# One chip, two blocks of a network: the statistics between a block's end and the next, taken together, and the second attention's ends reordered

## What is computed

```python
def rmsnorm_2(x, g):
    xf = x.astype(jnp.float32)
    y = xf * lax.rsqrt(jnp.mean(xf * xf, axis=-1, keepdims=True) + EPS)
    return (y * g.astype(jnp.float32)).astype(x.dtype)
...
    h = rmsnorm_2(x, g_pre[l, 0]) * (1 + sc1) + sh1
    x = x + 0.5 * gt1 * rmsnorm_2(swiglu(h, w_gu1[l], w_dn1[l]), g_post[l, 0])

    h = rmsnorm_2(x, g_pre[l, 1]) * (1 + sc2) + sh2
    y = token_mixer(h, w_in[l], w_a2[l], b_a[l], b_f[l], g_gla[l], w_pa[l], w_pb[l], w_out[l])
    x = x + gt2 * rmsnorm_2(y, g_post[l, 1])

    h = rmsnorm_2(x, g_pre[l, 2]) * (1 + sc3) + sh3
    x = x + 0.5 * gt3 * rmsnorm_2(swiglu(h, w_gu2[l], w_dn2[l]), g_post[l, 2])
```

## Time and profile before

| | |
|---|---|
| median of 3 runs | 2352.78 us (2352.03 to 2357.11) |
| profiled execution, its own time | 2360.18 us |
| span in the profile, mean granted clock | 2358.0 us, 0.982 |
| PE busy | 2306.4 us, 98% |
| DVE, ACT, POOL busy | 42%, 38%, 44% |
| DMA | 263.95 MB, mean 112 GB/s |

### The profile page before, as it was taken

The page is one execution under the profiler, slowest core; times in us unless marked ns, Lnnn a source line. Parts: engine busy times, 40 slices in busy tenths (PEclk is TensorE's granted clock), DMA queues, the critical chain, the costliest instruction groups (busy, mean ns, idle before and its releaser), DMA issues.

```text
span 2358.0 us, 33517 instructions
## 1 busy us (share of the span) xinstructions
PE 2306.4 (98%) x10816; PEld 1904.4 (81%) x10816; DVE 982.0 (42%) x1616; ACT 897.8 (38%) x1621; POOL 1041.5 (44%) x792
## 2 busy tenths in 40 slices
PE   8999999999999999999999999999999899999997
PEld 7888888888888888888888778888677688888886
DVE  6899885446514214100113135555765425110112
ACT  4334653333222333332332354445555443332331
POOL 3455653454444443444454443333222353444443
PEclk8999999999999999999998999999999999999998
DMA  4333443338837532333332223335112431333331
GB/s 150 93 98 103 144 131 123 99 115 296 270 94 243 154 89 77 97 98 94 98 94 59 81 81 113 108 111 173 53 52 59 139 94 54 94 98 98 94 98 58
DMA packets 129338, 263.95 MB, mean 112 GB/s; under 512 B 14240, under 2 KB 14368, under 8 KB 128608
## 3 DMA queue, kind: packets, MB, share of 16 engines
q1 hardware_dynamic: 119520, 236.51, 33.7%
q10 hardware_dynamic: 9728, 26.25, 2.9%
HBM read 250.02 MB, written 12.58 MB: 111 GB/s over the span
## 4 chain that ended last, share of the span: by engine, by line
PE 67%; issue 19%; POOL 8%; DVE 4%; ACT 1%; DMA 0%; POOLq 0%; ACTq 0%; DVEq 0%
PE bank L973 22%; PE bank L974 21%; PE bank L975 21%; POOL wlo L406 8%; PE bank L1084 1%; DVE bank L1591 1%; PE bank L1108 1%; DVE G L1764 1%; DVE G L1774 1%; PE bank L1048 0%; PE bank L1092 0%; PE bank L1068 0%; DMA cols<-d_cols 0%; DVE bank L1662 0%; PE bank L1076 0%
## 5 line engine op out<-in xcount | busy, mean ns | idle before, releaser
L406 POOL TENSOR_TENSOR wlo<-raw,whi 128x512 fp32r<-128x512 f32 x750 | 992.5, 1329 | 1219.9 <-ACT whi L478 1219.0
L973 PE MATMUL bank<-a_hi,whi 128*128 128x512 f32 x1928 | 763.3, 396 | 10.2 <-POOL wlo L406 8.4
L975 PE MATMUL bank<-a_lo,whi 128*128 128x512 f32 x1928 | 751.9, 390 | 0.0
L974 PE MATMUL bank<-a_hi,wlo 128*128 128x512 f32 x1928 | 751.5, 390 | 0.0
L478 ACT ACTIVATE whi<-raw 128x512 fp32r<-128x512 f32 x750 | 468.9, 627 | 706.4 <-PE bank L975 629.2
L973 PEld LDWEIGHTS bank<-a_hi,whi 128*128 128x128 f32 x1928 | 362.7, 188 | 91.6 <-POOL wlo L406 10.0
L975 PEld LDWEIGHTS bank<-a_lo,whi 128*128 128x128 f32 x1928 | 362.6, 188 | 76.5
L974 PEld LDWEIGHTS bank<-a_hi,wlo 128*128 128x128 f32 x1928 | 363.0, 188 | 75.8 <-issue 1.4
L973 PE MATMUL bank<-b_hi,whi 128*128 128x512 f32 x852 | 336.1, 394 | 0.6 <-DVE b_lo L1729 0.3
L974 PE MATMUL bank<-b_hi,wlo 128*128 128x512 f32 x852 | 332.5, 390 | 0.0
L975 PE MATMUL bank<-b_lo,whi 128*128 128x512 f32 x852 | 332.5, 390 | 0.0
(11 more groups left out here) (245 smaller groups left out, 1860.9 us busy)
## 6 DMA issues: line engine op xcount, KB each, us to landing
raw<-d_stream SPq DMA_DIRECT2D x750, 256.0 KB, 2.6
G<-d_ada SPq DMA_DIRECT2D x72, 512.0 KB, 4.6
spill_rv<-tmp ACTq DMA_DIRECT2D x32, 256.0 KB, 2.0
G<-spill_rv ACTq DMA_DIRECT2D x6, 1024.0 KB, 7.3
G<-d_x ACTq DMA_DIRECT2D x4, 512.0 KB, 5.5
spill_ga<-sq ACTq DMA_DIRECT2D x8, 256.0 KB, 3.7
G<-spill_ga ACTq DMA_DIRECT2D x1, 2048.0 KB, 8.2
G<-d_x ACTq DMA_DIRECT2D x1, 2048.0 KB, 13.4
```

The source lines that it names most:

```text
L406: pool.tensor_tensor(wlo[:, s % SRING, :], raw[:, s % RING, :], whi[:, s % SRING, :].bitcast(F32), ALU.subtract).then_inc(lo_done, 1)
L973: pe.matmul(out_ps, w_hi, hi[:, k, :], start=first and q == 0, stop=False)
L974: pe.matmul(out_ps, w_lo, hi[:, k, :], start=False, stop=False)
L975: mm = pe.matmul(out_ps, w_hi, lo[:, k, :], start=False, stop=last and q == len(ks) - 1)
```

## The change

With y scaled by a per-feature weight w and by the root r1 of its own norm, the new x is x + r1 w y. The sum of its squares over the features is S(x x) + 2 r1 S(x w y) + r1 r1 S(w y w y). So the kernel after takes three sums while y's tiles come: S(y y) as before, S(x w y) and S(w y w y); S(x x) it keeps from the turn before (`X_SUM`). Per tile there are a second square on ACT (`weighted_square`) and on DVE a product and two additions (`cross`). PE sums six tiles of 512 positions into `AUX` and bank 6 (`sums_between`), and `roots` makes both roots, one behind the other. PE broadcasts both (`two_roots`), and `next_block` adds the residual and makes the operands in one loop over k. `residual` stays for the last block. `add_pairs`, the squares of x and the sums over pairs are gone in both turns.

At the start of the second attention the products for the second half (`by_r(1)`) move behind the first `tmp`, the first quotients from m = 3 to m = 6, and `qk_half(15)` from m = 5 to m = 7. At its end the gate loads are cut into halves, the first issued behind the last scores instead of the last output, and `tick("pb")` goes ahead of the waits and the sigmoids.

```diff
-        SQ8, PAIRS, SQ_FIRST = tiles(8 * T, KD), tiles(16 * T, 4), tiles(S0, KD)
+        SQ_FIRST = tiles(S0, KD)
         SQ_ACC = tmp[:, 1, :]
+        CA, BA, CROSS, GSQ = G[:, 8 * T:9 * T], G[:, 9 * T:10 * T], tiles(10 * T, 2), tiles(12 * T, 2)
+        X_SUM, ROOT1, ROOT2, SUM_T = small[:, 5, 8:12], small[:, 4, 8:12], small[:, 4, 12:16], small[:, 6, 8:12]
...
-            def add_pairs(norm):
-                for j in range(4):
-                    pool.wait_ge(sq_ready, 8 * norm + 2 * j + 2)
-                    pool.tensor_tensor(PAIRS[:, j, :], SQ8[:, 2 * j, :], SQ8[:, 2 * j + 1, :], ALU.add)\
-                        .then_inc(pair_ready, 1)
             def add_up(norm, k):
...
                 else:
                     to = PLAN[stage][0] + (AHEAD if at else 0)
                     low_run(at, to)
-                    if norm != "n1":
-                        add_pairs(NORM[norm])
                     at = to
...
+            def weighted_square(b, m):
+                if m > 1:
+                    act.wait_ge(gsq_added, 6 * b + max(m - 2, 1))
+                act.activation(GSQ[:, m % 2, :], Y[:, m, :], ACT.Square, scale=derived[:, 3 + b, m:m + 1])\
+                   .then_inc(gsq_ready, 1)
             def round_a(fill, val, shift=None, name=None):
...
                     if norm is not None:
                         wait_evac(act, name, 0, m)
                         square(norm, m, (X if norm in (NORM["n2"], NORM["nf"]) else Y)[:, m, :])
+                    if norm == NORM["post1"]:
+                        weighted_square(0, m)
             def ffn(n, norm):
...
             ffn(2, NORM["post1"])
-            for k in range(KD):
-                act.wait_ge(x_ready, KD + k + 1)
-                pair_square(k, X[:, k, :])
...
                         wait_used(act, "qkb", 0, 31)
                     operand_hi(s - (STEPS - 7))
+            act.wait_ge(fox_s, UNITS)
+            act.dma_start(GB2[:, 4:8, :], spill_rv[:, 3 * KD:3 * KD + 4, :]).then_inc(ld_b2[0], 16)
             act.wait_ge(fox_o, STEPS)
-            act.dma_start(GB2[:, 4:8, :], spill_rv[:, 3 * KD:3 * KD + 4, :]).then_inc(ld_gb, 16)
-            act.dma_start(GB2[:, 0:4, :], spill_rv[:, 3 * KD + 4:4 * KD, :]).then_inc(ld_gb, 16)
-            act.dma_start(GA2[:, :, :], spill_rv[:, 2 * KD:3 * KD, :]).then_inc(ld_ga, 16)
+            act.dma_start(GA2[:, 0:4, :], spill_rv[:, 2 * KD:2 * KD + 4, :]).then_inc(ld_g2[0], 16)
             operand_hi(KD - 1)
-            act.wait_ge(ld_ga, 32)
-            act.wait_ge(ld_gb, 32)
+            act.dma_start(GB2[:, 0:4, :], spill_rv[:, 3 * KD + 4:4 * KD, :]).then_inc(ld_b2[1], 16)
+            act.dma_start(GA2[:, 4:8, :], spill_rv[:, 2 * KD + 4:3 * KD, :]).then_inc(ld_g2[1], 16)
             for m in range(KD + 1):
                 if m < KD:
+                    tick("pb", 0, 2 * m)
+                    if m % 4 == 0:
+                        act.wait_ge(ld_g2[m // 4], 16)
+                        act.wait_ge(ld_b2[m // 4], 16)
                     act.activation(GA2[:, m, :], GA2[:, m, :], ACT.Sigmoid).then_inc(gate2, 1)
                     act.activation(gb2(m), gb2(m), ACT.Sigmoid).then_inc(gate2, 1)
-                    tick("pb", 0, 2 * m)
                 if m:
                     act.wait_ge(b_val, 2 * KD + m)
                     act.activation(b_hi[:, m - 1, :], tmp[:, (m - 1) % 2, :], ACT.Copy).then_inc(b_hi_w, 1)
...
                 act.activation(Y[:, m, :], bank_of("wout", m)[:, :], ACT.Copy).then_inc(evac_of("wout", m), 1)
                 wait_evac(act, "wout", 0, m)
                 square(NORM["post2"], m, Y[:, m, :])
-            for k in range(KD):
-                act.wait_ge(x_ready, 2 * KD + k + 1)
-                pair_square(k, X[:, k, :])
+                weighted_square(1, m)
             round_a("hf3", 40, lambda k: mods[:, 48 + k:49 + k], "gu3a")
...
+                for tt in range(4):
+                    mm = pe.matmul(sums[:, at + tt:at + tt + 1], value[:, tt * P:(tt + 1) * P], ones[:, 0:1],
+                                   start=first and tt == 0, stop=tt == 3, skip_group_check=True)
+                return mm
+            def sums_between(b, norm):
+                pe.wait_ge(sq_summed, 8 * norm + KD - 1)
+                sum_at(AUX, 0, SQ_ACC, True)
+                pe.wait_ge(cross_ready, 3 * b + 2)
+                sum_at(bank[6], 0, BA, True)
+                sum_at(bank[6], 4, CA)
+                pe.wait_ge(sq_ready, 8 * norm + KD)
+                sum_at(AUX, 0, sq[:, (KD - 1) % 2, :]).then_inc(sq_summed, 1)
+                pe.wait_ge(cross_ready, 3 * b + 3)
+                sum_at(bank[6], 4, CROSS[:, (KD - 1) % 2, :])
+                pe.wait_ge(gsq_ready, KD * (b + 1))
+                sum_at(bank[6], 0, GSQ[:, (KD - 1) % 2, :]).then_inc(between, 1)
+            def two_roots(n):
+                keep_warm(12)
+                broadcast(n, src=ROOT1)
+                keep_warm(14)
+                broadcast(n + 1, src=ROOT2, dst=bank[6])
+                keep_warm(22)
...
                     sum_both(KD - 1)
+                elif n == 2:
+                    sums_between(0, norm)
                 else:
                     sum_up(norm)
...
-            broadcast(7, warm=8)
-            keep_warm(26)
-            sum_pairs(1, "pre2")
-            broadcast(8, warm=8)
-            keep_warm(10)
+            two_roots(7)
             def row_panel(name, i, k, ops):
...
                     scores(1)
-                if m < 6:
-                    qk_half(10 + m)
+                if m < 5 or m == 7:
+                    qk_half(10 + min(m, 5))
             pe.wait_ge(ld_v, 32)
...
             stage8("pb", OPA, opa, FILL_A["ob"], 2)
             for m in range(KD):
                 tile8("wout", 0, m, OPB, opb, FILL_B["merged"], m == 0)
-            sum_up(NORM["post2"])
-            broadcast(9, warm=8)
-            keep_warm(26)
-            sum_pairs(2, "pre3")
-            broadcast(10, warm=8)
-            keep_warm(10)
+            sums_between(1, NORM["post2"])
+            two_roots(9)
             ffn(3, NORM["post3"], False, FILL_A["hf3"])
             broadcast(11)
...
                         in1=cols[:, COLS["g_post_2"][0] + 8 * b:COLS["g_post_2"][0] + 8 * b + 8], op0=ALU.mult, op1=ALU.mult))
                 own.next(dve.tensor_tensor(derived[:, 6, :], derived[:, 0, :],
                                            cols[:, COLS["norm_f_g"][0]:COLS["norm_f_g"][0] + KD], ALU.mult))
+            def cross(b, name, m):
+                wait_evac(dve, name, 0, m)
+                z = dve.scalar_tensor_tensor(out=CROSS[:, m % 2, :], in0=Y[:, m, :], scalar=derived[:, 3 + b, m:m + 1],
+                                             in1=X[:, m, :], op0=ALU.mult, op1=ALU.mult)
+                if m == KD - 1:
+                    z.then_inc(cross_ready, 1)
+                    return
+                own.next(z)
+                if m:
+                    last = m == KD - 2
+                    both = dve.tensor_tensor(CA, CROSS[:, 0, :] if m == 1 else CA, CROSS[:, m % 2, :], ALU.add)
+                    if last:
+                        both.then_inc(cross_ready, 1)
+                    else:
+                        own.next(both)
+                    dve.wait_ge(gsq_ready, KD * b + m + 1)
+                    dve.tensor_tensor(BA, GSQ[:, 0, :] if m == 1 else BA, GSQ[:, m % 2, :], ALU.add)\
+                       .then_inc(gsq_added, 1)
+                    dve.wait_ge(gsq_added, 6 * b + m)
+                    if last:
+                        dve.memset(small[:, 6, 12:13], 0.0).then_inc(cross_ready, 1)
             def ffn(n, with_ada):
...
                         wait_used(dve, name, 0, ((m + 1) * K - 1) // 4)
                         dve.tensor_tensor(acc[:, m, :], acc[:, m, :], bank_of(name, m)[:, :], ALU.add)\
                            .then_inc(evac_of(name, m), 1)
+                        if n == 2:
+                            cross(0, name, m)
             dve.memset(ones[:, :], 1.0).then_inc(vchain, 1)
...
             own.next(dve.tensor_tensor(sum2, sum2, r1, ALU.mult))
+            own.next(dve.tensor_copy(X_SUM, sum2))
...
-            def modulated(b, fill):
-                operand_a(fill, lambda k: derived[:, b, k:k + 1], lambda k: mods[:, 24 * b + k:24 * b + k + 1])
+            def roots(b, norm):
+                dve.wait_ge(sq_summed, 8 * (norm + 1))
+                rsqrt(AUX[:, 0:4], 4, 1.0 / D, st_ready, ROOT1)
+                stat[0] += 1
+                dve.wait_ge(st_ready, stat[0])
+                dve.wait_ge(between, b + 1)
+                own.next(dve.tensor_tensor(SUM_T, bank[6][:, 0:4], ROOT1, ALU.mult))
+                own.next(dve.scalar_tensor_tensor(out=SUM_T, in0=bank[6][:, 4:8], scalar=2.0, in1=SUM_T, op0=ALU.mult,
+                                                  op1=ALU.add))
+                own.next(dve.tensor_tensor(SUM_T, SUM_T, ROOT1, ALU.mult))
```

(66 more changed lines are left out.)

15 lines of the change are left out of this document (8 added, 7 removed).

## The result

| | before | changed |
|---|---|---|
| median of 5 runs | 2353.12 us (2352.03 to 2357.11) | 2341.25 us (2340.96 to 2342.64) |
| ratio, 95% interval | | 0.9945 [0.9934, 0.9956] |
| span of the profiled execution | 2358.0 us | 2339.1 us |

The kernel is faster by 11.9 us; 17.9 was forecast, and 2341.25 lies in the range. The spans differ by 18.9 us, more than the medians: the changed kernel's profiled execution reaches the first turn 4.65 us earlier (first sum at 1261.28 instead of 1265.93), and of this 4.64 are there at the first tile of dn2b (DVE's add at 1215.32 instead of 1219.96), ahead of the change's first work on a tile. Up to turn one the clock lay at 0.5 for 17.1 us, in the kernel before for 27.3, and half of the difference is 5.1. So the places of the change are compared each from its own start.

A forecast was written before the change was run, and what follows sets the result against it. The chain that ended last went 67% through TensorE (PE), so time was to be won where PE stops or does work outside the product. 5.1 + 2.8 + 8.0 + 2.2 - 0.2 = 17.9 us off 2352.8 gave 2335, range 2327 to 2344.

The forecast's parts named there:

- pb, 8.0: Start of pb: PE's 6.64 us wait for POOL goes, plus 1.4 of half clock; 8.0 us, bounds 3.7 and 8.2.
- Turn one, 5.1: Turn between dn2b and qka, with the first qka pass behind it: 5.1 us returned.
- Δ: Time from a turn's first sum to its second broadcast in the changed kernel, forecast at 16.5 us.
- my 2.5: Part of Δ: PE's loss to half clock in a turn, taken as 2.5 us, bounds 0 and 5.1.
- my 14.0: Part of Δ: PE's sums, warming matmuls and two broadcasts in a turn, 14.0 us at full clock.
- clock at 0.5 into the product: Sign of being wrong: the clock still at 0.5 when PE is in the product matmuls behind a turn.
- Turn two, 2.8: Turn between wout and gu3a, with the first pass behind it: 2.8 us returned.
- the rival in which the clock eats the turns: Clock at 0.5 for 10 us per turn; turns return 2.5 and 0.2, total 12.7, 2340 us; chance 0.14.
- the 7.9: Both turns together, as predicted: 7.9 us (5.1 and 2.8).
- The start, 2.2: Start of the second attention: turned(0) starts at 1663.1 instead of 1665.2; 2.2 us, bounds 0 and 3.6.
- The slower rival: POOL and DVE block each other, POOL feeds PE too late in wout and dn2b; 2375 us, chance 0.03.
- 2.5 per operation: Time in us per POOL operation from which the slower rival's blocking in wout and dn2b decides.

The follow-up runs named there:

- e3: Kernel before with only the end of the second attention changed (gate loads in halves, tick("pb") ahead of the waits): 2346.62 us, ratio 0.9966.
- e2: Changed kernel with both ends of the second attention as before, so the two turns alone: 2350.35 us, ratio 0.9984 against the kernel before.
- e1: Kernel before with the changes at both ends of the second attention alone, turns as before: 2347.43 us, ratio 0.9968.
- e4: Kernel before with only the order at the second attention's start changed: 2353.15 us, ratio 0.9992 [0.9983, 1.0001].
- e10: e6 with the additions x + y of each turn moved from DVE to POOL: 2340.51 us, ratio 0.9941 against the kernel before.
- e6: Changed kernel with keep_warm(12) and keep_warm(14) ahead of the broadcasts cut to 2 each: 2331.11 us, ratio 0.9903 against the kernel before.
- e9: e6 with five warming matmuls ahead of operands 6 and 7 of tile 0: 2329.41 us, ratio 0.9891 against the kernel before.

## Why the prediction was right, and where its sizes were off

Its ways held; the sum was 5 to 6 us too large. By the pair of traces 4.3 of that lie in the turns and 1.4 in the attention's start, and pb gave 0.8 more than forecast.

**pb, 8.0.** From the attention's last 16 matmuls into the heads' bank to the first sum of turn two it took 97.6 us before and 88.8 after: 8.8 (in e3 88.8 too), and e3's time gives 8.0. The wait went, the clock stayed up (1.00 at 1843.2 to 1853.0), and panel 5 was not late.

**Turn one, 5.1; measured 3.7** (52.9 less 49.2). Δ was forecast at 16.5 and measured at 16.5, which is luck in part. Inside it the clock's share was larger than my 2.5 (6.8 us at half clock lose 3.4), and the rest, 13.1, smaller than my 14.0. The last a_lo ended 21.9 behind the broadcast, as forecast (22.05). The term that is missing is a fall inside the pass, which PE's waits of about 1.2 us brought on: 3.4 us at half clock, 1.4 to 1.7. I had named these waits, but priced the pass behind them at full clock, though "clock at 0.5 into the product" stood among my signs of being wrong, and it came in both passes.

**Turn two, 2.8; measured -0.1 in this pair** (64.3 less 64.5). Δ was 18.1 (the sums' last 16 matmuls took 3.55 instead of 2.71, with the clock at 0.5 for 10.2 us), 1.6 over; the fall in the pass took another 1.4 to 1.7. Together they cover the 2.9 that are missing. So in this pair the rival in which the clock eats the turns held in turn two. But the pair is not the rule. In e2 turn two has 6.8 us at half clock, Δ is 16.5, and it takes 62.8. The means over the six executions above are 65.3 with the old turns and 63.6 with the changed, a gain of 1.7, and for turn one 52.4 and 48.4, a gain of 4.0. By these the turns return 5.7 of the 7.9, by the times 3.8 (e2) or 5.4 (the whole change less e1).

**The start, 2.2; measured 0.8.** From the first transpose to turned(1) it took 19.8 us before and 19.0 after, and e4 can't tell its gain from nothing. It is the same 0.8 in e1 and e4. The wait of 1.69, which the prediction puts before turned(0), stands before turned(1). The third transpose's wait went as forecast. But at two tiles DVE's b_lo lies beside POOL and takes 1.71 instead of 0.68, tmp(5) makes PE wait 1.82 us, and the quotients, now behind it, hold turned(0) by 1.65. The half clock at 1654.8 stayed in this execution; where it was gone (e4), the next quotient held PE instead.

**The slower rival** (POOL and DVE block each other until PE starves in dn2b and wout) did not come. Its mechanism is real: DVE's new additions took 1.71 us in the mean, a_lo in e10 1.58. It slowed POOL too, whose timeline in wout reads:

```profile
1906.26 1.29 POOL L431 TENSOR_TENSOR tmp<-tmp,sq 128x512 f32<-128x512 f32 x1 [0.67 <-ACT sq L485]
1907.51 3.44 POOL L411 TENSOR_TENSOR wlo<-raw,whi 128x512 fp32r<-128x512 f32 x2
```

Two low halves took 3.44 there, 1.7 each, and 2.55 in the kernel before. With the addition POOL needs 4.7 of the 5.44 us of a tile, where the prediction had 5.0 and 2.5 per operation was the point from which it decides. PE waited for POOL nowhere in dn2b or wout.

**What the prediction did not ask** was whether keep_warm(12) and (14) earned their place. It counted them at 6.2 us at full clock per turn as given; e6 shows that cutting them to 2 returns 10 us over both turns and costs no clock.

**Slips that change no sum.** The prediction names 3.4 us at half clock in turn one of before, where there are 13.6. PE's own end of the pass is 5.2 + 21.5 = 26.7 behind the broadcast, not 27.1, and the gates' 4 MB from 1855.3 to 1867.5 are 3.05 us per MB, not 2.9. A panel is 12 matmuls, as the prediction counts it, and not the 24 of the section on the kernel before.

Open: why the falls differ from one execution to the next (the changed kernel had two ahead of turn one, the kernel before four; e2 lacks one behind the same waits), what keep_warm(22) is worth, and e9's one run of 3447.77. A better order for POOL in e10 was not tried.

## What to carry to other kernels

When matmuls are issued to warm the clock, look at what is queued behind them: if it is a broadcast that another engine waits for, they are on the path, and the granted clock of that stretch shows whether they return anything. When a serial stretch is shortened, price the pass behind it anew: here the operands, at 2.71 us each, became the limit, and the short waits cost the clock as well as themselves. When the clock differs from one execution to the next, read a stretch in more than one before its gain is believed: turn two gave -0.1 in one pair and 1.7 in the mean of six. Work moved to an idle engine is not free if it shares a port with the engine that it relieves.
